# First loads of the down stage issued earlier, and the norm of its output reordered, in a one-layer hybrid decoder step

## The reference, cut to what matters

```python
g = h @ w_gate;  u = h @ w_up                       # (t, 1024) @ (1024, 2816)
gp = concat([conv_prev, g], axis=1)
gc = sum(gp[:, j:j + t] * w_conv[j] for j in range(3)) + b_conv
a = gelu(gc) * u
f = a @ w_down                                      # (t, 2816) @ (2816, 1024)
x = x + f * rsqrt(mean(f * f, axis=-1) + 1e-6) * norm_ffn_post
conv_out = gp[:, -2:]                               # the last two rows of g, per sequence
```

## Time and profile before

| | us |
|---|---|
| median of three runs (lowest, highest) | 3407.99 (3403.71, 3416.47) |
| the profiled execution | 3398.65 |
| its span, first to last instruction | 3397.0 |
| ffn_up, first to last matmul | 1879.4 to 2793.1 |
| ffn_down, barrier to end | 2797.8 to 3397.0 |

### The profile page before, as it was taken

The page is one execution under the profiler, slowest core; times in us unless marked ns, Lnnn a source line. Parts: engine busy times, 40 slices in busy tenths (PEclk is TensorE's granted clock), DMA queues, the critical chain, the costliest instruction groups (busy, mean ns, idle before and its releaser), DMA issues. The chain is left out here.

```text
span 3397.0 us, 57191 instructions
## 1 busy us (share of the span) xinstructions
PE 3075.3 (91%) x19779; PEld 2849.7 (84%) x19779; DVE 2317.5 (68%) x4537; ACT 1773.5 (52%) x3913; POOL 716.0 (21%) x535
## 2 busy tenths in 40 slices
PE   6989989799989997877799799999999988999997
PEld 5989989698989895444587799999999988999886
DVE  7787776577768873332796888888888864454444
ACT  5545544588867773322444555655566544443332
POOL 4464554254510003332453100000000000000000
PEclk7999999899999998998899899999999999999999
DMA  4556446727257668998454444454444538778853
GB/s 140 152 158 192 157 153 188 198 50 167 60 136 177 165 187 264 325 316 255 161 191 142 148 157 139 138 170 143 151 138 137 163 115 273 252 228 256 258 169 102
DMA packets 579154, 600.31 MB, mean 177 GB/s; under 512 B 37370, under 2 KB 478803, under 8 KB 573715
## 3 DMA queue, kind: packets, MB, share of 16 engines
q1 hardware_dynamic: 553540, 531.49, 52.8%
q0 software_dynamic: 19104, 63.06, 5.8%
q10 hardware_dynamic: 6224, 2.12, 0.3%
HBM read 481.71 MB, written 181.84 MB: 195 GB/s over the span
## 5 line engine op out<-in xcount | busy, mean ns | idle before, releaser
L3087 PE MATMUL fd_d<-fd_ah,fd_wh 128*128 128x416 f32 x880 | 319.2, 363 | 50.4 <-DVE fd_wl L3179 46.5
L2886 PE MATMUL fu_x<-fu_oh,fu_wh 128*128 128x352 f32 (+1 forms) x1056 | 341.9, 324 | 14.2 <-DVE fu_gb L2769 6.1
L2886 PE MATMUL fu_x<-fu_oh,fu_wl 128*128 128x352 f32 (+1 forms) x1056 | 340.8, 323 | 0.0
L2886 PE MATMUL fu_x<-fu_ol,fu_wh 128*128 128x352 f32 (+1 forms) x1056 | 338.2, 320 | 0.0
L3087 PE MATMUL fd_d<-fd_ah,fd_wl 128*128 128x416 f32 x880 | 313.1, 356 | 0.0
L3087 PE MATMUL fd_d<-fd_al,fd_wh 128*128 128x416 f32 x880 | 311.0, 353 | 0.0
L2755 DVE TENSOR_TENSOR fu_wl<-fu_sm,fu_wh 128x512 fp32r<-128x512 f32 x264 | 181.8, 689 | 69.0 <-ACT fu_wh L2651 67.0
L1009 DVE CUSTOM_DVE_ANT_0 aa_p<-aa_sc,aa_bias 128x512 f32<-128x512 f32 (+3 forms) x320 | 188.5, 608 | 57.4 <-PE aa_sc L935 42.0
L3087 PEld LDWEIGHTS fd_d<-fd_ah,fd_wh 128*128 128x128 f32 x880 | 167.7, 191 | 61.1 <-DVE fd_wl L3179 53.3
L2886 PEld LDWEIGHTS fu_x<-fu_oh,fu_wh 128*128 128x128 f32 x1056 | 199.0, 188 | 18.4 <-issue 11.7
L3202 DVE COPY fd_yn<-fd_t 32x128 f32<-32x128 f32 x40 | 11.2, 279 | 287.6 <-PE fd_t L3061 287.6
(11 more groups left out here) (342 smaller groups left out, 9174.6 us busy)
## 6 DMA issues: line engine op xcount, KB each, us to landing
bx_kca<-in_cache_a_k SPq DMA_DIRECT2D x128, 256.0 KB, 13.7
sa_vca<-in_cache_a_v POOLq DMA_DIRECT2D x128, 256.0 KB, 7.8
out<-in_cache_win_k SPq DMA_DIRECT2D x64, 511.0 KB, 6.4
out<-in_cache_win_v SPq DMA_DIRECT2D x64, 511.0 KB, 6.4
fd_wr<-in_w_down SPq DMA_DIRECT2D x80, 384.0 KB, 6.3
fd_wr<-in_w_down SPq DMA_DIRECT2D x80, 320.0 KB, 7.6
pj_ra<-in_w_in SPq DMA_DIRECT2D x36, 512.0 KB, 5.6
pj_rb<-in_w_in SPq DMA_DIRECT2D x36, 512.0 KB, 4.6
```

The costliest lines, as they stand in the source:

```text
L2886: m = pe.matmul(bank[:, 0:n], w[:, k - 1, c], o[:, k - 1, c, 0:n], start=k in (5, 2, 1) and c == 0 and x == 0, stop=c == HC - 1 and x == 2 ...
L3087: m = pe.matmul(dp[T % 2][:, 0:FG], w[:, j, c], a[:, p % RING, c], start=j == 0 and c == 0 and x == 0, stop=j == SLOTS - 1 and c == size - ...
```

## The change

Six edits.

1. **Early loads.** `load_down_values` and `load_down_weights` are new functions on module level. In `ffn_up`, at step q = 52 (the ninth of the last round), SP waits for the tokens' last low part and then issues seven transfers: the first two parts of the values, the four weight parts of tile 0, and the norm weights. Their buffers (wr, gain over the token sums ts; ar, state, junk over the tokens) move into `Kept`. They stand ahead of `send(48)` and of `load_w(55, 1)` in the queue. `ffn_down` starts without them.
2. **Ring positions.** The values' ring starts at slot 3 (`slot_of`), so that parts 0 and 1 don't lie where the last sends of `ffn_up` still read; ACT waits for these before part 2. Value part 0 is cut into pieces of 1, 2 and 3 chunks (before: 2 and 4).
3. **ACT order.** `squares(T - 1)` and `root` come ahead of the wait for the tile's last matmul; the squares read the transposed tile in PSUM. `turn_back` waits for the squares two tiles back.
4. **DVE order.** `normalise` and `keep_state` (a tile later than before) come ahead of `keep_turned(T)`.
5. **Norm weights.** `keep_turned` multiplies by them on the way out of PSUM (tensor_tensor in place of copy). `normalise` is then one scalar_tensor_tensor (times root, plus residual) in place of two instructions; the two separate additions at the end go. The stores' semaphore becomes two.
6. **No POOL sums.** In round 0 of `ffn_up` the token sums 6, 7 and 4 move from POOL to DVE, and the sums' order is 5, 6, 7, 4 in all rounds.

The diff, cut to its core:

```diff
+def load_down_weights(eng, t, keep, n):
+    T, j = divmod(n, SLOTS)
+    c0, d = D_FIRST[j], T % DC
+    src = t["w_down"].rearrange("(c p) f -> p c f", p=P)
+    eng.dma_start(keep.wr[:, j, 0:D_PARTS[j]], src[:, c0:c0 + D_PARTS[j], d * P:(d + 1) * P]).then_inc(keep.w_in[j], 16)
+
+def load_down_values(eng, t, keep, p):
+    g, j = divmod(p, SLOTS)
+    if j == 0:
+        rounds = sum(at_ < (g + 1) * FG for at_, _ in ROUNDS)
+        for u in range(2):
+            eng.wait_ge(keep.a_out[u], 16 * PAIRS * rounds)
+    c0 = D_FIRST[j]
+    eng.dma_start(keep.ar[:, p % 2, 0:D_PARTS[j]],
+                  t["a"][:, c0:c0 + D_PARTS[j], g * FG:(g + 1) * FG]).then_inc(keep.ar_in[p % 2], 16)
...
                 if q % FNQ == 3 and q // FNQ + 1 < NR:
                     load_tokens(q // FNQ + 1)
+                if q == (NR - 1) * FNQ + 8:
+                    sp.wait_ge(t_lo, raised(7 * NR))
+                    for p in range(2):
+                        load_down_values(sp, t, keep, p)
+                    for n in range(SLOTS):
+                        load_down_weights(sp, t, keep, n)
+                    sp.dma_start(keep.gain[:], t["norm_ffn_post"].partition_broadcast(P)).then_inc(keep.gain_in, 16)
                 if q % 2 == 0 and q >= 4:
                     send(q - 4)
...
-            token_sum(pool, 0, 7)
-            token_sum(pool, 0, 6)
-            token_sum(pool, 0, 4)
...
-                if k == 2:
-                    token_sum(dve, 0, 5)
+                if k in (2, 3):
+                    token_sum(dve, 0, 5 if k == 2 else 6)
...
                 if i in EARLY:
+                    token_sum(dve, 0, EARLY[i])
                     tokens_low(0, EARLY[i])
...
-        PIECES = [(0, 0, 2), (0, 2, 6)] + [(p, 0, D_PARTS[p % SLOTS]) for p in range(1, PARTS)]
+        PIECES = [(0, 0, 1), (0, 1, 3), (0, 3, 6)] + [(p, 0, D_PARTS[p % SLOTS]) for p in range(1, PARTS)]
...
+        def slot_of(p):
+            return (p + 3) % RING
...
-            load_a(0)
-            load_w(0)
-            load_w(1)
-            load_a(1)
-            load_w(2)
-            load_w(3)
-            sp.dma_start(gain[:], t["norm_ffn_post"].partition_broadcast(P)).then_inc(gain_in, 16)
             load_a(2)
             load_a(3)
...
                 if T >= 2:
                     pe.wait_ge(y_ok, raised(T - 1))
+                    pe.wait_ge(y_sq, raised(T - 1))
...
+                if p == 2:
+                    for u in range(2):
+                        act.wait_ge(keep.a_out[u], 16 * PAIRS * NR)
...
-                    m = act.activation(junk[0:r, b], yn[0:r, g % 2, b, d * P:(d + 1) * P], ACT.Square,
+                    m = act.activation(junk[0:r, b], tp[T % 2][0:r, b * P:(b + 1) * P], ACT.Square,
                                        accum_out=s4[0:r, b, d:d + 1])
...
                 weights_high(SLOTS * T + 5)
+                if T >= 1:
+                    squares(T - 1)
+                if d == 0 and g >= 1:
+                    root(g - 1)
                 act.wait_ge(mm, raised(SLOTS * T + SLOTS))
                 if T >= 1:
                     act.wait_ge(y_turned, raised(T))
                 act.activation(yT[:], dp[T % 2][:, 0:FG], ACT.Copy).then_inc(d_read, 1)
-                if T >= 1:
-                    squares(T - 1)
-                if d == 0 and g >= 1:
-                    root(g - 1)
...
-                dve.tensor_copy(yn[0:r, g % 2, FB - 1, c], tp[k][0:r, (FB - 1) * P:])
-                dve.tensor_copy(yn[:, g % 2, 0:FB - 1, c],
-                                tp[k][:, 0:(FB - 1) * P].rearrange("p (b x) -> p b x", b=FB - 1)).then_inc(y_ok, 1)
+                dve.tensor_tensor(yn[0:r, g % 2, FB - 1, c], tp[k][0:r, (FB - 1) * P:], gain[0:r, c], ALU.mult)
+                dve.tensor_tensor(yn[:, g % 2, 0:FB - 1, c], tp[k][:, 0:(FB - 1) * P].rearrange("p (b x) -> p b x", b=FB - 1),
+                                  gain[:, c].rearrange("p (o x) -> p o x", o=1).to_broadcast([P, FB - 1, P]),
+                                  ALU.mult).then_inc(y_ok, 1)
...
-                dve.scalar_tensor_tensor(y, y, s4[0:r, b, DC + 2:DC + 3], gain[0:r], ALU.mult, ALU.mult).then_inc(y_norm, 1)
-                if not (g == NF - 1 and b >= 2):
-                    dve.wait_ge(y_norm, raised(FB * g + b + 1))
+                if g == NF - 1 and b >= 2:
+                    dve.wait_ge(end_in, raised(32))
+                    x = x_end[b - 2][0:r].bitcast(F32)
+                else:
                     dve.wait_ge(x_in[b % 2], 16 * (FB // 2 * g + b // 2 + 1))
-                    dve.tensor_tensor(y, y, xt[0:r, b % 2], ALU.add).then_inc(y_add, 1)
+                    x = xt[0:r, b % 2]
+                dve.scalar_tensor_tensor(y, y, s4[0:r, b, DC + 2:DC + 3], x, ALU.mult, ALU.add).then_inc(y_add, 1)
...
-                if T < TILES - 1:
-                    keep_turned(T)
                 if g >= 1 and d < FB:
                     normalise(g - 1, d)
-                if g == NF - 1 and 1 <= d < 1 + STATES:
-                    keep_state(d - 1)
-            keep_turned(TILES - 1)
+                if g == NF - 1 and 2 <= d:
+                    keep_state(d - 2)
+                keep_turned(T)
```

More of the change, by code:

```diff
@@ L2391, with __init__ @@
 class Kept:
-    def __init__(self, outer):
+    def __init__(self, outer, ahead):
         self.carry = outer.sb("carry", [P, FT, 2])
@@ L3022, in _ @@
             sp.wait_ge(last_out, raised(16 * (2 + FB)))
-            sp.wait_ge(y_out, 16 * FB * (NF - 1))
+            for i in range(2):
+                sp.wait_ge(y_out[i], 16 * FB * (NF // 2))
             sp.wait_ge(keep.rolled, 16 * len(ROLLS))
@@ L3319, in program @@
         with Stage(nc, "fk") as last:
-            keep = Kept(last)
+            keep = Kept(last, ahead)
             ffn_up(nc, t, ahead, keep)
```

121 lines of the change are left out of this document (55 added, 66 removed).

## The result

| | us |
|---|---|
| before, median of four runs (lowest, highest) | 3405.85 (3398.0, 3416.47) |
| after, median of four runs (lowest, highest) | 3367.54 (3364.12, 3369.96) |
| ratio after to before (95% interval) | 0.9889 (0.9862 to 0.9916) |
| the profiled execution of after, its span | 3369.96, 3368.3 |

The forecast was 3366, with the range 3350 to 3386 and 0.92 on faster. The change is 1.1% faster, by some 38 us, and lies in the range. PE's busy time on the page is as good as the same as before, so the gain is in its waits and at the ends.

What follows compares the result with a forecast made beforehand. PE, busy 91% of the span, was taken as the bound, so time returns only where it waits or does not run. -38 -4.8 -10 +12 +0 = -41 us from the median 3408 gave 3367, stated as 3366; range 3350 to 3386.

Steps and rivals of the forecast that it cites:

- DVE's order: ffn_down's tiles: norm and state copies moved into DVE's wait before the transposes, 38 us saved.
- what is late next: ffn_down's tiles: next late is DVE's low part for part 2, ready at 5.8 us, asked for at 6.7.
- The cover: ffn_down's tiles: 0.9 us between part 2's low part being ready and PE asking, hiding a dearer product.
- Rival C: ffn_down's tiles: low part for part 2 later by 1.4 us, 19 us lost, 3386; chance 0.20.
- D: ffn_down's tiles: rival with the product out of PSUM 2.4 us dearer than the copy, slower, 3425; chance 0.02.
- ACT's order: ffn_down's tiles: 1.3 us of squares a tile move ahead of ACT's wait; nothing lost.
- The end: End of ffn_down: four DVE instructions stay of eight, 4.8 us saved, bounds 4.0 and 5.3.
- First loads, the gain: Start of ffn_down: part 2's value transfer issued 9.4 us earlier, gain 10 us, bounds 8.5 and 11.5.
- First loads, the cost: ffn_up, step 52: 4.31 MB of loads delay a send and PE waits; cost 12 us, bounds 0 and 16.
- the clock: ffn_up after PE's wait at step 52: PE at 1.2 in place of 2.4 GHz, 1.6 us.
- POOL sums: ffn_up, round 0: 8.9 us of stretched DVE instructions gone, sums and waits added; 0, bounds -3 and +3.
- The sum: Whole kernel: -38 -4.8 -10 +12 +0 = -41 us, 3356 for the span.

Runs made afterwards that it cites:

- runs 4 and 5: Two kernels against the changed one: old program orders on ACT and DVE restored, 3387.56 us; norm weights not multiplied out of PSUM, norm in two instructions again, 3369.27 us.
- extra4: The changed kernel with the product with the norm weights out of PSUM repeated four times more in each tile, each with a wait: 3429.41 us.
- run 10: Early loads behind the sends, round 0's sums ahead, second value load two tiles later: 3347.16 us; the same with ACT's old order: 3355.65 us.
- no_early_loads: The changed kernel with the early loads issued at the start of ffn_down, in the old order: 3366.32 us.
- burst_behind: The changed kernel with step 52's sends and copy of old cache rows issued ahead of the seven early loads instead of behind them: 3350.09 us.
- the six: Six kernels with the same ffn_up, the changed kernel among them; ffn_up took 927.9 to 929.6 us in them, 928.6 in the mean.
- run 2: The changed kernel with only the two value loads ahead of the sends at step 52, weight loads and norm weights behind: 3367.80 us.
- pool_sums: The changed kernel with three token sums of round 0 on POOL again, sums in the order 5, 7, 6, 4: 3370.88 us.
- act_late: The changed kernel with only ACT's order undone, squares and root behind the copy of the finished tile: 3376.35 us.
- behind_ahead: The changed kernel with early loads behind step 52's sends and, in round 0, sums ahead of the tokens' low parts: 3344.07 us.

## Why the prediction was right, point by point

**DVE's order, -38.** Measured -35.5, and the mechanism as said: the periods of tiles with a norm are those of tiles without, the last group's 13.84 (forecast 13.9). By the periods of before the order was worth 38.6 us; against that stand two things. 1.5 us are late weights at tiles 11 and 19: "what is late next" was sought on DVE and not on SP's queue, where DVE's stalls had covered a slow transfer. And every tile's 66 matmuls take 12.52 us in place of 12.47, in all kernels with the change; over 38 periods that is 1.7 us. Why wasn't settled. The working gave the gain to edits 4 and 5 together; the square of runs 4 and 5 gives it to the orders, edit 5 adds nothing there. Had the norm stayed in its old place, edit 5 would have brought half of it by itself (18.2 us).

**The cover, 0.9.** Measured 0.89 and 0.90. The product costs no more than the copy did. Rival C needed 1.4 us and D 2.4; with D's price in place, extra4 did end on the other side. The forecast's slope, one for one over 39 tiles, held.

**ACT's order, 0.** Right by the pieces, also in that four microseconds are left in a group's first tile: in the profiled execution late squares used them up without a loss. The medians of the kernels with late squares leave it open (run 10).

**The end, -4.8.** Measured -4.7.

**First loads, the gain, -10.** Measured -9.5 (after) and -9.2 (against no_early_loads).

**First loads, the cost, +12.** Mechanism and place right, the size too small: 14.0 (burst_behind) to 14.9 us (no_early_loads) against the mean of the six, 15.0 to 15.9 against after alone, inside the bound of 16. The delay sits in SP's issuing rather than behind the packets (run 2), which the working had not told apart, but its size was right: 12.1 us of DVE's wait where 11.7 were worked out. PE's wait was 11.46 us where 10.7 were. The mis-sized term is the clock: 1.6 us were taken from a wait of 2.1 us, after 11.5 us of idle time it was 2.5. 11.46 and 2.5 make the 14.0.

**POOL sums, 0.** No difference beyond the spread (928.4 us in pool_sums, 927.9 to 929.6 with the sums on DVE), within the bounds of 3. The three waits of 1.4 us for ACT came as forecast. That ACT's order puts the copy of a product behind a sum, so that PE waits 9.24 us at one place, was not seen; it happens to cost about what the two old waits did. Here the Trainium skill (SBUF — State Buffer, the section on the two sides of its ports) names an exclusive lock; the trace agrees (3.0 us lost by each of three instructions), but what came back in the end was not the lock's price, since the sums had to go somewhere.

**The sum.** -41 was forecast, and the pieces give -33.5 without the first mark's 4.9; the medians lie 38.3 apart, and their interval, 29 to 47 us, holds both. DVE's order fell short by 2.5 us, the start by 0.5, and ffn_up cost 4.2 more than forecast: 2.0 are the burst's by burst_behind, the rest is as small as the spread of that piece. All of it goes to the same side. So the mechanism and the range were right, but that the median came out within 2 us of 3366 is luck: the sum expected some 7 us more gain than the pieces show, and the scatter of the executions covered it.

## What to carry to other kernels

A burst of prefetches costs where it stands ahead of something that is waited for, and there roughly by its bytes: put behind the store that another engine is about to wait for, the same 4.31 MB were free here. Before an instruction is moved or added, read its cover as the distance between its end and the time at which the consumer asks; up to there it costs nothing, beyond it one for one in every tile. And when a stall goes, look for the next late thing on the transfer queues too, not only on the engine that was late.

## What the runs showed of the hardware that was not expected

After 11.5 us without a matmul, TensorE ran 20 matmuls at the lower clock (0.28 us apart in place of 0.155) before the higher one was granted (after). With two value loads of 2.34 MB and two copies in front, one tile's weights took 12.4 to 15.0 us to land where PE waited for them (12.74 in after, 13.01 in act_late, 15.02 in behind_ahead), and a whole tile lasts 12.95. SyncE's issue of a weight load took 0.56 us behind one value load (no_early_loads) and 1.9 to 2.2 us behind 2.3 to 3.1 MB (no_early_loads, after), so that what stands behind it is delayed before it is even in the queue.
